# Last stage of a one-core decoder layer: a buffer for every tile, mixer tiles read during the stage before, one scaling on ScalarE

## The chip, the cores and the metric

The kernel runs on one NeuronCore of a Trainium2 chip. The metric is the device time of one execution in microseconds (us). The profile is one further execution with the hardware profiler on.

## The reference, cut to what matters

The program is one decoder layer over 2048 tokens of 1024 float32 numbers: a token mixer (pooling and dilated attention) and then a mixture of experts. Only the very end of it is touched:

```
# h: normalised rows after the mixer; x: the residual stream after the mixer
y = zeros(T, D).at[slot_tok].add(expert_out[slot] * slot_w[slot])   # two slots per token
x = x + gt_f * (y * rsqrt(mean(y * y, -1) + 1e-6) * g_post_ffn)
```

Each token has two experts, so two rows of the experts' output, each with its own share. The last stage fetches the two rows, adds them with their shares, normalises the sum, scales it by a row of 1024 numbers and adds the mixer's result.

## The kernel before

`build` calls the stages one after another; each stage is a scope that ends by clearing its semaphores and with a barrier of all engines. The last three are `route`, `experts` and `combine`. Intermediates lie in DRAM: `x1_dram` ("x_mixed", the residual stream after the mixer, 8.39 MB), `h_dram`, and `y_dram` ("y_slots", 64 blocks of 128 expert output rows, of which a run-time table says how many are used). `x1_dram` is written in the stage before `route`.

`experts` works block by block on 128 rows of one expert. Its weights come in 12 parts (`PARTS = 12`, of which `GU = 8` are gate/up parts) into `raw_gu` and `raw_d`, 12 times 128 x 1024 float32. ScalarE and VectorE cut each part into a high and a low half (L1479, L1485); when the low half of part g is done, `lo_ready[g]` goes up and SyncE may load the next expert's part over the raw one. When SyncE has issued the last expert's weights, it writes zeros to the unused blocks of `y_dram` (L1509) and waits until they have landed. ScalarE stores each block's output (L1639).

`combine` works on 16 tiles of 128 tokens with three buffers (`BUF = 3`) for each kind of tile:

- GpSimd gathers the two expert rows of each token into `yy[:, t % 3, 0]` and `yy[:, t % 3, 1]` by two indirect DMAs of 128 rows of 4 KB (L1730). From tile 3 on it first waits until VectorE has mixed tile t - 3.
- SyncE loads the row `mod` (broadcast to 128 partitions) and, two tiles ahead, the mixer's tile into `x1[:, t % 3]` (L1741). From tile 3 on this waits until the store out of that same buffer has landed. In its one queue the load of tile t + 2 stands ahead of the store of tile t (L1749).
- VectorE's `mix(t)` scales the first row by its share (L1769, tensor_scalar) and adds the second (L1771, scalar_tensor_tensor). Then for each tile: `mix(t + 1)`, the reciprocal of the root (L1780), the scaling by it and by `mod` (L1782), and the sum with the mixer's tile, written into `x1` (L1786).
- ScalarE squares the mixed tile with an accumulated sum (L1760) and takes the root (L1762).

The two lines that hold the waits in question:

```
if t >= BUF: pool.wait_ge(mixed, t - BUF + 1)                   # GpSimd, ahead of a tile's two gathers
if t >= BUF: sp.wait_ge(stored[t % BUF], 16 * (t // BUF))       # SyncE, ahead of a load of x1
```

Of the kernel before, what the change touches and what calls it, by code (L numbers as in the profile page):

```python
# [5 lines left out]
P = 128  # L6
D = 1024
SEQ = 2048
KD = D // P
TILES = SEQ // P  # L10
# [10 lines left out]
NE = EG * EPG  # L21
DE = 512
KE = DE // P
NB = 64
EPS = 1e-6

F32 = mybir.dt.float32
F32R = mybir.dt.float32r
I32 = mybir.dt.int32
ALU = mybir.AluOpType  # L30
ACT = mybir.ActivationFunctionType
AX = mybir.AxisListType
ds = bass.ds
# [913 lines left out]
NR = EG + NE  # L947
# [266 lines left out]
H2 = DE // 2  # L1214
GU, PARTS = 8, 12


def route(nc, logits, dest, share, table, slot_rows, raw_gu, raw_d, w_gate, w_up, w_down):


# [195 lines left out]
                dve.wait_ge(rows_ready, 1)  # L1416


def experts(nc, table, slot_rows, ident, h_dram, raw_gu, raw_d, w_gate, w_up, w_down, y_dram):

# [2 lines left out]
    with ExitStack() as ctx:  # L1425
# [22 lines left out]
        lo_taken = [s.sem(f"lo_taken{i}") for i in range(2)]  # L1448
        silu_ready = [s.sem(f"silu_ready{i}") for i in range(2)]
        hid_ready = [s.sem(f"hid_ready{i}") for i in range(2)]  # L1450
        row_ready, row_seen, all_stored, zeroed, rest_zeroed, y_ready = (s.sem(n) for n in (
            "row_ready", "row_seen", "all_stored", "zeroed", "rest_zeroed", "y_ready"))

        def entry(eng, r, b, top):
            return eng.value_load(table[0:1, r, ds(b, 1)], min_val=0, max_val=top)
# [31 lines left out]
        with nc.Block() as block:  # L1487
            @block.sync
            def _(sp):
                def load(e, before):  # L1490

                    for g in range(PARTS):
                        sp.wait_ge(lo_ready[g], before)
                        load_part(sp, g, e, raw_gu, raw_d, w_gate, w_up, w_down, part_loaded[g])

                for g in range(PARTS):
                    sp.sem_inc(part_loaded[g], 32 if g < GU else 16)  # L1497

                def reload(b):
                    with sp.If(entry(sp, 1, b, 1) > 0):  # L1500
                        load(entry(sp, 0, b, NE - 1), entry(sp, 2, b, NE))

                count = by_twos(sp, lambda i: [reload(2 * i), reload(2 * i + 1)])

                sp.wait_ge(zeroed, 1)
                with sp.Fori(0, NB // 2) as i:
                    with sp.If(2 * i >= count):
                        for u in range(2):
                            sp.dma_start(y_dram[ds((2 * i + u) * P, P), :], zero[:, :]).then_inc(rest_zeroed, 16)  # L1509
                    with sp.Else():  # L1510
                        sp.sem_inc(rest_zeroed, 32)
                sp.wait_ge(rest_zeroed, 16 * NB)

            @block.gpsimd
# [186 lines left out]
                by_twos(dve, lambda i: [block_of(2 * i, 0), block_of(2 * i + 1, 1)])  # L1701


def combine(nc, dest, share, y_dram, x1_dram, gate_dram, out):

    BUF = 3
    with ExitStack() as ctx:
        s = Scope(nc, ctx, "comb")
        yy = s.sb("yy", [P, BUF, 2, D])
        x1 = s.sb("x1", [P, BUF, D])  # L1710
        y = s.sb("y", [P, BUF, D])
        sq = s.sb("sq", [P, D])
        mod = s.sb("mod", [P, D])
        eps = s.sb("eps", [P, 1])
        ms, root, rstd = s.sb("ms", [P, 2]), s.sb("root", [P, 2]), s.sb("rstd", [P, 2])
        gathered = [s.sem(f"gathered{i}") for i in range(BUF)]
        x_loaded = [s.sem(f"x_loaded{i}") for i in range(BUF)]
        stored = [s.sem(f"stored{i}") for i in range(BUF)]
        mod_loaded, eps_ready, first, mixed, squared, rooted, recips, scaled, summed = (s.sem(n) for n in (
            "mod_loaded", "eps_ready", "first", "mixed", "squared", "rooted", "recips", "scaled", "summed"))  # L1720
        with nc.Block() as block:
            @block.gpsimd
            def _(pool):
                pool.memset(eps[:, :], EPS).then_inc(eps_ready, 1)  # L1724

                for t in range(TILES):
                    if t >= BUF:
                        pool.wait_ge(mixed, t - BUF + 1)
                    for c in range(2):
                        pool.indirect_dma_start(out=yy[:, t % BUF, c, :], out_offset=None, in_=y_dram,  # L1730
                                                in_offset=bass.IndirectOffsetOnAxis(ap=dest[:, c, t:t + 1], axis=0)
                                                ).then_inc(gathered[t % BUF], 16)

            @block.sync
            def _(sp):
                sp.dma_start(mod[:, :], gate_dram.partition_broadcast(P)).then_inc(mod_loaded, 16)

                def load(t):
                    if t >= BUF:
                        sp.wait_ge(stored[t % BUF], 16 * (t // BUF))  # L1740
                    sp.dma_start(x1[:, t % BUF, :], x1_dram[ds(t * P, P), :]).then_inc(x_loaded[t % BUF], 16)  # L1741

                load(0)
                load(1)
                for t in range(TILES):
                    if t + 2 < TILES:
                        load(t + 2)
                    sp.wait_ge(summed, t + 1)
                    sp.dma_start(out[0, ds(t * P, P), :], x1[:, t % BUF, :]).then_inc(stored[t % BUF], 16)  # L1749
                for i in range(BUF):  # L1750
                    sp.wait_ge(stored[i], 16 * len(range(i, TILES, BUF)))

            @block.scalar
            def _(act):
                act.wait_ge(eps_ready, 1)
                for t in range(TILES):
                    act.wait_ge(mixed, t + 1)
                    if t >= 2:
                        act.wait_ge(recips, t - 1)
                    nc.scalar.activation(sq[:, :], y[:, t % BUF, :], ACT.Square, accum_out=ms[:, t % 2:t % 2 + 1]).then_inc(squared, 1)  # L1760
                    act.wait_ge(squared, t + 1)
                    nc.scalar.activation(root[:, t % 2:t % 2 + 1], ms[:, t % 2:t % 2 + 1], ACT.Sqrt, scale=1.0 / D,  # L1762
                                         bias=eps[:, 0:1]).then_inc(rooted, 1)

            @block.vector
            def _(dve):
                def mix(t):
                    dve.wait_ge(gathered[t % BUF], 32 * (t // BUF + 1))
                    dve.tensor_scalar(y[:, t % BUF, :], yy[:, t % BUF, 0, :], share[:, 0, t:t + 1], None, ALU.mult).then_inc(first, 1)  # L1769
                    dve.wait_ge(first, t + 1)  # L1770
                    dve.scalar_tensor_tensor(out=y[:, t % BUF, :], in0=yy[:, t % BUF, 1, :], scalar=share[:, 1, t:t + 1],  # L1771
                                             in1=y[:, t % BUF, :], op0=ALU.mult, op1=ALU.add).then_inc(mixed, 1)

                dve.wait_ge(mod_loaded, 16)
                mix(0)
                for t in range(TILES):
                    if t + 1 < TILES:
                        mix(t + 1)
                    dve.wait_ge(rooted, t + 1)
                    dve.reciprocal(rstd[:, t % 2:t % 2 + 1], root[:, t % 2:t % 2 + 1]).then_inc(recips, 1)  # L1780
                    dve.wait_ge(recips, t + 1)
                    dve.scalar_tensor_tensor(out=y[:, t % BUF, :], in0=y[:, t % BUF, :], scalar=rstd[:, t % 2:t % 2 + 1],  # L1782
                                             in1=mod[:, :], op0=ALU.mult, op1=ALU.mult).then_inc(scaled, 1)
                    dve.wait_ge(scaled, t + 1)
                    dve.wait_ge(x_loaded[t % BUF], 16 * (t // BUF + 1))
                    dve.tensor_tensor(x1[:, t % BUF, :], y[:, t % BUF, :], x1[:, t % BUF, :], ALU.add).then_inc(summed, 1)  # L1786


def build(nc, x, c, w_ada, b_ada, g_pre_mix, g_post_mix, g_pre_ffn, g_post_ffn, w_in, w_pool_group, pool_scale,
# [13 lines left out]
    with ExitStack() as ctx:  # L1803
        def top(name, shape, dt=F32):
            return ctx.enter_context(nc.sbuf_tensor(name, shape, dt))
# [10 lines left out]
        merge(nc, proj, att, ident, w_pool_group, pool_scale, w_branch_pool, w_branch_att, merged)  # L1816
        dest, share = top("dest", [P, 2, TILES], I32), top("share", [P, 2, TILES])
        table, slot_rows = top("table", [1, 4, NB + 1], I32), top("slot_rows", [P, NB + 2], I32)
        with nc.sbuf_tensor("logits", [P, TILES, NR], F32) as logits:
            mix_out(nc, x, merged, w_out, ada_part, b_ada, (g_post_mix, g_pre_ffn, g_post_ffn), ident, w_group_router,  # L1820
                    w_expert_router, b_group_router, b_expert_router, gate_dram, x1_dram, h_dram, logits)
            with nc.sbuf_tensor("raw_gu", [P, GU, 2, 2, H2], F32) as raw_gu, nc.sbuf_tensor("raw_d", [P, KE, D], F32) as raw_d:
                route(nc, logits, dest, share, table, slot_rows, raw_gu, raw_d, w_exp_gate, w_exp_up, w_exp_down)
                experts(nc, table, slot_rows, ident, h_dram, raw_gu, raw_d, w_exp_gate, w_exp_up, w_exp_down, y_dram)
        combine(nc, dest, share, y_dram, x1_dram, gate_dram, out)


# [21 lines left out]
```

## Time and profile before

| | |
|---|---|
| time, median of 3 (lowest to highest) | 2801.63 us (2801.57 to 2801.66) |
| the profiled execution: its own time | 2803.04 us |
| its span, from first to last instruction | 2801.3 us |
| `combine` in it | from 2679 to 2801.3 us, 122 us |
| last expert output stored (issued) | 2672.6 us |

The span is the trace's time axis: 0 is the first instruction. The time of an execution is 1.7 us more than its span here. An engine's idle time is put down to whatever released it last; a load or a store "lands" when its last byte is there. DMA share is the mean busy share of the core's 16 DMA engines.

### The profile page before, as it was taken

To read this page: it belongs to the slowest core of one execution; us is meant where nothing else is said; L and a number is where in the kernel's file an instruction comes from. 1 tells how busy PE (TensorE), PEld (TensorE's weight loads), DVE (VectorE), ACT (ScalarE), POOL (GpSimd) and SP (SyncE) were. 2 spreads that over 40 slices of the span, in tenths; PEclk is the share of its full clock that TensorE was granted. 3 is DMA by queue.
4 is the path that set the end of the run, shared out by engine and by line. 5 is a ranking of instruction groups with operands and counts; after the bars stand their busy time and mean duration, and the time that the engine had idled before them with its cause. 6 is when DMAs were issued, how large, how long until landed. Compare 5 with 4: busy or idle time off the path is not lost. (4 is left out here: it accounts for less than half of the span.)

```text
span 2801.3 us, 39203 instructions
## 1 busy us (share of the span) xinstructions
PE 2397.4 (86%) x13485; PEld 2056.7 (73%) x13486; DVE 1365.5 (49%) x1700; ACT 917.5 (33%) x1509; POOL 474.8 (17%) x311
## 2 busy tenths in 40 slices
PE   3599999999999888868959983999999999999910
PEld 3488888888888677846848873888889889889910
DVE  6552111122323177646424447886664756466346
ACT  3200000000000055433322221886664755565321
POOL 2311111111111101022335541010010100010032
PEclk9799999999999999769979995999999999999955
DMA  6112212132332423255554433998975876678468
GB/s 224 46 60 90 75 60 75 60 111 102 132 124 101 162 99 109 81 166 200 200 197 158 151 135 127 368 375 300 323 258 207 289 272 231 240 254 296 184 224 270
DMA packets 293164, 499.73 MB, mean 178 GB/s; under 512 B 21337, under 2 KB 226673, under 8 KB 283506
## 3 DMA queue, kind: packets, MB, share of 16 engines
q1 hardware_dynamic: 269778, 414.05, 43.1%
q0 software_dynamic: 11808, 43.00, 4.6%
q10 hardware_dynamic: 11520, 41.95, 3.8%
q8 instruction: 32, 0.52, 0.1%
q14 instruction: 26, 0.21, 0.0%
HBM read 383.37 MB, written 115.54 MB: 178 GB/s over the span
## 5 line engine op out<-in xcount | busy, mean ns | idle before, releaser
L349 PE MATMUL proj_psum<-h_hi,proj_w_hi 128*128 128x512 f32 x1216 | 481.8, 396 | 19.1 <-POOL proj_w_lo L334 19.1
L350 PE MATMUL proj_psum<-h_lo,proj_w_hi 128*128 128x512 f32 x1216 | 481.6, 396 | 0.0
L351 PE MATMUL proj_psum<-h_hi,proj_w_lo 128*128 128x512 f32 x1216 | 481.4, 396 | 0.0
L1546 PE MATMUL moe_p_gu<-moe_hi_gu,moe_xT_hi 128*128 128x256 f32 x1536 | 440.5, 287 | 1.7 <-DVE moe_xT_lo L1660 1.7
L369 DVE COPY proj_out<-proj_psum 128x512 f32<-128x512 f32 x152 | 123.7, 815 | 635.3 <-PE proj_psum L351 634.1
L1547 PE MATMUL moe_p_gu<-moe_lo_gu,moe_xT_hi 128*128 128x256 f32 x1536 | 432.6, 282 | 0.0
L1548 PE MATMUL moe_p_gu<-moe_hi_gu,moe_xT_lo 128*128 128x256 f32 x1536 | 432.5, 282 | 0.0
L1485 DVE TENSOR_TENSOR moe_lo_gu<-raw_gu,moe_hi_gu 128x1024 fp32r<-128x1024 f32 x256 | 301.5, 1219 | 23.8 <-ACT moe_hi_gu L1479 17.4
L327 ACT ACTIVATE proj_w_hi<-proj_raw 128x1024 fp32r<-128x1024 f32 x38 | 40.3, 1061 | 781.9 <-PE proj_psum L351 772.2
L1546 PEld LDWEIGHTS moe_p_gu<-moe_hi_gu,moe_xT_hi 128*128 128x128 f32 x1536 | 290.5, 189 | 4.2 <-issue 2.1
L1547 PEld LDWEIGHTS moe_p_gu<-moe_lo_gu,moe_xT_hi 128*128 128x128 f32 x1536 | 290.7, 189 | 2.1
L1548 PEld LDWEIGHTS moe_p_gu<-moe_hi_gu,moe_xT_lo 128*128 128x128 f32 x1536 | 290.6, 189 | 0.0
L349 PEld LDWEIGHTS proj_psum<-h_hi,proj_w_hi 128*128 128x128 f32 x1216 | 228.9, 188 | 74.7 <-issue 19.5
L1479 ACT ACTIVATE moe_hi_gu<-raw_gu 128x1024 fp32r<-128x1024 f32 x256 | 256.5, 1057 | 41.1 <-SPq L1497 41.1
L350 PEld LDWEIGHTS proj_psum<-h_lo,proj_w_hi 128*128 128x128 f32 x1216 | 228.9, 188 | 55.4
L351 PEld LDWEIGHTS proj_psum<-h_hi,proj_w_lo 128*128 128x128 f32 x1216 | 228.9, 188 | 55.4
L334 POOL TENSOR_TENSOR proj_w_lo<-proj_raw,proj_w_hi 128x1024 fp32r<-128x1024 f32 x38 | 98.2, 2585 | 724.6 <-ACT proj_w_hi L327 724.6
L1546 PE MATMUL moe_p_y<-moe_hi_d,moe_hT_hi 128*128 128x512 f32 x384 | 159.4, 415 | 34.9 <-DVE moe_hT_lo L1660 34.9
L1681 DVE TENSOR_TENSOR moe_hid<-moe_p_gu,moe_act_g 128x256 f32<-128x256 f32 x96 | 40.6, 423 | 264.9 <-ACT moe_act_g L1621 264.2
L1518 POOL COPY moe_row<-slot_rows 128x1 int32 (+1 forms) x50 | 30.6, 612 | 801.2 <-PE moe_p_turn L1537 787.4
L1548 PE MATMUL moe_p_y<-moe_hi_d,moe_hT_lo 128*128 128x512 f32 x384 | 151.7, 395 | 0.0
L1547 PE MATMUL moe_p_y<-moe_lo_d,moe_hT_hi 128*128 128x512 f32 x384 | 151.5, 394 | 0.0
(261 smaller groups left out, 3791.9 us busy)
## 6 DMA issues: line engine op xcount, KB each, us to landing
raw_gu<-in_w_exp_gate SPq DMA_DIRECT2D x256, 256.0 KB, 6.3
raw_gu<-in_w_exp_up SPq DMA_DIRECT2D x256, 256.0 KB, 7.7
raw_d<-in_w_exp_down SPq DMA_DIRECT2D x128, 512.0 KB, 9.1
projected<-proj_out SPq DMA_DIRECT2D x38, 1024.0 KB, 4.3
y_slots<-moe_ys ACTq DMA_DIRECT2D x48, 512.0 KB, 6.4
proj_raw<-in_w_in SPq DMA_DIRECT2D x38, 512.0 KB, 6.2
att_qkv<-projected SPq DMA_DIRECT2D x18, 1024.0 KB, 8.4
proj_w_rest<-in_w_ada SPq DMA_DIRECT2D x8, 2048.0 KB
```

Of the source, the lines that this page charges most:

```text
L327: nc.scalar.activation(w_hi[:, u, :, :], raw[:, u, :, :], ACT.Copy).then_inc(hi_ready[u], 1)
L334: pool.tensor_tensor(w_lo[:, u, :, :], raw[:, u, :, :], w_hi[:, u, :, :], ALU.subtract).then_inc(lo_ready[u], 1)
L349: pe.matmul(bank, w_hi[:, u, k, :], h_hi[:, k, tok], start=(k == 0), stop=False)
L350: pe.matmul(bank, w_hi[:, u, k, :], h_lo[:, k, tok], start=False, stop=False)
L351: mm = pe.matmul(bank, w_lo[:, u, k, :], h_hi[:, k, tok], start=False, stop=(k == KD - 1))
L369: ins = dve.tensor_copy(view[:, ds(tg * per, per), :], psum[:, u, tg, :].rearrange("p (m r) -> p m r", r=dilation))
L1479: nc.scalar.activation(hi_part(g), raw_part(g), ACT.Copy).then_inc(hi_ready[g], 1)
L1485: dve.tensor_tensor(lo_part(g), raw_part(g), hi_part(g), ALU.subtract).then_inc(lo_ready[g], 1)
L1546: pe.matmul(bank, x_hi, w_hi, start=first, stop=False)
L1547: pe.matmul(bank, x_hi, w_lo, start=False, stop=False)
L1548: return pe.matmul(bank, x_lo, w_hi, start=False, stop=last)
L1681: dve.tensor_tensor(hid[:, half, :], p_gu[:, half, 1, 0:H2], act_g[:, half, :], ALU.mult).then_inc(hid_ready[half], 1)
```

## The change

1. `combine` holds all 16 tiles of gathered rows at once: `yy` is `[P, TILES, 2, D]`. GpSimd issues its 32 gathers without any wait. Each gather has a semaphore of its own. The buffers `y` are gone: everything is computed in place in `yy[:, t, 0]`, and the output is stored from there.
2. The mixer's tiles 0 to 11 are loaded in `experts`, by SyncE, after its zero blocks are issued, each into one of the 12 raw weight parts and each after the last expert's cut of that part (`lo_ready[g]`). SyncE leaves the stage when they have landed. `raw_gu`, `raw_d` (and `logits`) stay allocated to the end. Only tiles 12 to 15 (`LATE = 4`) are loaded in `combine`, at its start, into buffers of their own.
3. The first scaling (share 0) moves from VectorE to ScalarE as a Copy activation with a scale per partition, issued one tile ahead, ahead of the square of the tile before.
4. The constant `eps` is set by VectorE and not by GpSimd. `ms`, `root` and `rstd` have one column per tile. The one store semaphore is waited on once, at the end.

```
+def x1_part(t, raw_gu, raw_d):
+    return raw_gu[:, t, :, :, :].rearrange("p m k f -> p (m k f)") if t < GU else raw_d[:, t - GU, :]
...
 # experts, SyncE
+                cut = entry(sp, 2, NB, NE) + 1
+                for g in range(PARTS):
+                    sp.wait_ge(lo_ready[g], cut)
+                    sp.dma_start(x1_part(g, raw_gu, raw_d), x1_dram[ds(g * P, P), :]).then_inc(x1_loaded, 16)
+                sp.wait_ge(x1_loaded, 16 * PARTS)
                 sp.wait_ge(rest_zeroed, 16 * NB)
...
 # combine, GpSimd
-                pool.memset(eps[:, :], EPS).then_inc(eps_ready, 1)
                 for t in range(TILES):
-                    if t >= BUF:
-                        pool.wait_ge(mixed, t - BUF + 1)
                     for c in range(2):
-                        pool.indirect_dma_start(out=yy[:, t % BUF, c, :], out_offset=None, in_=y_dram,
+                        pool.indirect_dma_start(out=yy[:, t, c, :], out_offset=None, in_=y_dram,
                                                 in_offset=bass.IndirectOffsetOnAxis(ap=dest[:, c, t:t + 1], axis=0)
-                                                ).then_inc(gathered[t % BUF], 16)
+                                                ).then_inc(gathered[t][c], 16)
...
 # combine, SyncE
-                load(0)
-                load(1)
+                for t in range(LATE):
+                    sp.dma_start(x1[:, t, :], x1_dram[ds((PARTS + t) * P, P), :]).then_inc(x_loaded[t], 16)
                 for t in range(TILES):
-                    if t + 2 < TILES:
-                        load(t + 2)
                     sp.wait_ge(summed, t + 1)
-                    sp.dma_start(out[0, ds(t * P, P), :], x1[:, t % BUF, :]).then_inc(stored[t % BUF], 16)
+                    sp.dma_start(out[0, ds(t * P, P), :], yy[:, t, 0, :]).then_inc(stored, 16)
...
 # combine, ScalarE
+                def weight(t):
+                    act.wait_ge(gathered[t][0], 16)
+                    nc.scalar.activation(yy[:, t, 0, :], yy[:, t, 0, :], ACT.Copy, scale=share[:, 0, t:t + 1]).then_inc(first, 1)
+
                 act.wait_ge(eps_ready, 1)
+                weight(0)
                 for t in range(TILES):
+                    if t + 1 < TILES:
+                        weight(t + 1)
                     act.wait_ge(mixed, t + 1)
...
 # combine, VectorE
                 def mix(t):
-                    dve.wait_ge(gathered[t % BUF], 32 * (t // BUF + 1))
-                    dve.tensor_scalar(y[:, t % BUF, :], yy[:, t % BUF, 0, :], share[:, 0, t:t + 1], None, ALU.mult).then_inc(first, 1)
+                    dve.wait_ge(gathered[t][1], 16)
                     dve.wait_ge(first, t + 1)
-                    dve.scalar_tensor_tensor(out=y[:, t % BUF, :], in0=yy[:, t % BUF, 1, :], scalar=share[:, 1, t:t + 1],
-                                             in1=y[:, t % BUF, :], op0=ALU.mult, op1=ALU.add).then_inc(mixed, 1)
+                    dve.scalar_tensor_tensor(out=yy[:, t, 0, :], in0=yy[:, t, 1, :], scalar=share[:, 1, t:t + 1],
+                                             in1=yy[:, t, 0, :], op0=ALU.mult, op1=ALU.add).then_inc(mixed, 1)
```

## Rows read from the trace of the kernel before

**Rows 1.** The page's first line: the profiled execution.

```profile
span 2801.3 us, 39203 instructions
```

**Rows 2.** The chain that ended last, from 2690 us: start, length, what.

```profile
by line: DMA out<-comb_x 78.8%; DMA comb_yy<-y_slots,dest 8.1%; DMA comb_x<-x_mixed 3.8%; SPq L1741 3.4%; DVE comb_x L1786 2.2%; DVE comb_y L1782 1.2%; DVE comb_y L1771 1.2%; ACT L1760 1.1%; ACT L1762 1.1%; ACT comb_sq L1760 1.0%; issue 1.0
...
2681.09 9.07 DMA comb_yy<-y_slots,dest
...
2796.49 1.23 DVE comb_x L1786
```

**Rows 3.** Busy time by stretch: each engine, granted clock, DMA share, GB/s.

```profile
2679.00:2690.00 11.00, 0.00 (x0) 0.00 (x0) 0.00 (x0) 0.00 (x0) 5.72 (x7) 0.50 0.88 328
2685.00:2690.00 5.00, 0.00 (x0) 0.00 (x0) 0.00 (x0) 0.00 (x0) 1.70 (x2) 0.50 1.02 397
2690.00:2780.00 90.00, 0.00 (x0) 0.00 (x0) 59.90 (x66) 22.67 (x44) 37.92 (x26) 0.50 0.88 292
2710.00:2715.00 5.00, 0.00 (x0) 0.00 (x0) 3.88 (x6) 1.44 (x3) 3.90 (x2) 0.50 0.95 363
2730.00:2780.00 50.00, 0.00 (x0) 0.00 (x0) 31.72 (x35) 10.11 (x21) 18.16 (x13) 0.50 0.92 304
2780.00:2801.30 21.30, 0.00 (x0) 0.00 (x0) 12.87 (x14) 2.89 (x6) 0.00 (x0) 0.50 0.62 198
```

**Rows 4.** DMA from 2679 us on: packets; issues, KB each, median us to landing.

```profile
DMA packets 9362, 34.10 MB, mean 277 GB/s; under 512 B 1040, under 2 KB 1040, under 8 KB 9360
...
comb_x<-x_mixed SPq DMA_DIRECT2D x16, 512.0 KB, 5.6
```

**Rows 5.** Waits from 2679 us on: us in total, times, longest.

```profile
POOL comb_yy L1730 <- DVE comb_y L1771: 43.7, 12, 8.2
DVE comb_x L1786 <- DMA comb_x<-x_mixed: 31.3, 13, 6.7
```

**Rows 6.** Waits of SyncE's queue from 2560 us on.

```profile
SPq L1741 <- DMA out<-comb_x: 82.7, 13, 10.3
```

**Rows 7.** Groups of instructions from 2690 us on.

```profile
L1771 DVE SCALAR_TENSOR_TENSOR comb_y<-comb_yy,share,comb_y 128x1024 f32<-128x1024 f32 x16 | 20.5, 1284 | 0.6
...
L1760 ACT ACTIVATE comb_sq<-comb_y 128x1024 f32<-128x1024 f32 x16 | 16.9, 1056 | 71.7 <-DVE comb_y L1771 71.7
```

**Rows 8.** VectorE in order of time, one tile without a wait.

```profile
2701.17 0.15 DVE L1780 RECIPROCAL comb_rstd<-comb_root 128x1 f32<-128x1 f32 x1
...
2703.82 0.75 DVE L1769 TENSOR_SCALAR comb_y<-comb_yy,share 128x1024 f32<-128x1024 f32 x1
2704.60 1.28 DVE L1771 SCALAR_TENSOR_TENSOR comb_y<-comb_yy,share,comb_y 128x1024 f32<-128x1024 f32 x1
2705.80 0.15 DVE L1780 RECIPROCAL comb_rstd<-comb_root 128x1 f32<-128x1 f32 x1
```

**Rows 9.** GpSimd in order of time: a gather's issue alone, and beside VectorE.

```profile
2681.09 0.94 POOL L1730 DMA_INDIRECT comb_yy<-y_slots,dest  x1 [0.30 <-issue]
...
2701.52 1.93 POOL L1730 DMA_INDIRECT comb_yy<-y_slots,dest  x1 [2.70 <-DVE comb_y L1771]
```

**Rows 10.** SyncE's, VectorE's, GpSimd's and ScalarE's last work in `experts`.

```profile
2605.54 18.82 SPq L1509 DMA_DIRECT2D y_slots<-moe_zero  x16
...
2616.68 4.62 DVE L1485 TENSOR_TENSOR moe_lo_d<-raw_d,moe_hi_d 128x1024 fp32r<-128x1024 f32 x4
...
2631.69 0.97 POOL L1521 DMA_INDIRECT moe_xg<-h_moe,moe_row  x1 [0.79 <-POOL moe_row L1518]
...
2640.91 1.09 ACT L1600 ACTIVATE moe_xT_hi<-moe_p_turn 128x512 fp32r<-128x512 f32 x2
...
2672.61 0.34 ACTq L1639 DMA_DIRECT2D y_slots<-moe_ys  x1
```

**Rows 11.** Busy time by stretch at the end of `experts`.

```profile
2620.00:2630.00 10.00, 10.00 (x83) 9.78 (x82) 3.86 (x7) 2.13 (x5) 0.00 (x0) 1.00 1.02 417
...
2628.00:2645.00 17.00, 17.00 (x123) 15.88 (x123) 2.74 (x6) 4.94 (x8) 1.15 (x2) 1.00 0.29 114
2645.00:2672.00 27.00, 26.29 (x177) 23.68 (x175) 4.07 (x9) 5.01 (x10) 1.15 (x2) 1.00 0.10 39
```

More of the change, by code:

```diff
@@ L1416, in _, with experts @@
                 dve.wait_ge(rows_ready, 1)
-def experts(nc, table, slot_rows, ident, h_dram, raw_gu, raw_d, w_gate, w_up, w_down, y_dram):
+def experts(nc, table, slot_rows, ident, h_dram, raw_gu, raw_d, w_gate, w_up, w_down, y_dram, x1_dram):
     with ExitStack() as ctx:
@@ L1450, in experts @@
         hid_ready = [s.sem(f"hid_ready{i}") for i in range(2)]
-        row_ready, row_seen, all_stored, zeroed, rest_zeroed, y_ready = (s.sem(n) for n in (
-            "row_ready", "row_seen", "all_stored", "zeroed", "rest_zeroed", "y_ready"))
+        row_ready, row_seen, all_stored, zeroed, rest_zeroed, y_ready, x1_loaded = (s.sem(n) for n in (
+            "row_ready", "row_seen", "all_stored", "zeroed", "rest_zeroed", "y_ready", "x1_loaded"))
         def entry(eng, r, b, top):
@@ L1701, in _, with combine @@
                 by_twos(dve, lambda i: [block_of(2 * i, 0), block_of(2 * i + 1, 1)])
-def combine(nc, dest, share, y_dram, x1_dram, gate_dram, out):
-    BUF = 3
+def combine(nc, dest, share, y_dram, x1_dram, gate_dram, raw_gu, raw_d, out):
+    LATE = TILES - PARTS
     with ExitStack() as ctx:
         s = Scope(nc, ctx, "comb")
-        yy = s.sb("yy", [P, BUF, 2, D])
-        x1 = s.sb("x1", [P, BUF, D])
-        y = s.sb("y", [P, BUF, D])
+        yy = s.sb("yy", [P, TILES, 2, D])
+        x1 = s.sb("x1", [P, LATE, D])
         sq = s.sb("sq", [P, D])
@@ L1714, in combine @@
         eps = s.sb("eps", [P, 1])
[L1715 to L1720, printed above, removed]
+        ms, root, rstd = s.sb("ms", [P, TILES]), s.sb("root", [P, TILES]), s.sb("rstd", [P, TILES])
+        gathered = [[s.sem(f"gathered{t}_{c}") for c in range(2)] for t in range(TILES)]
+        x_loaded = [s.sem(f"x_loaded{t}") for t in range(LATE)]
+        mod_loaded, eps_ready, first, mixed, squared, rooted, recips, scaled, summed, stored = (s.sem(n) for n in (
+            "mod_loaded", "eps_ready", "first", "mixed", "squared", "rooted", "recips", "scaled", "summed", "stored"))
         with nc.Block() as block:
@@ L1736, in _ @@
                 sp.dma_start(mod[:, :], gate_dram.partition_broadcast(P)).then_inc(mod_loaded, 16)
[L1738 to L1741, printed above, removed]
-                load(0)
-                load(1)
+                for t in range(LATE):
+                    sp.dma_start(x1[:, t, :], x1_dram[ds((PARTS + t) * P, P), :]).then_inc(x_loaded[t], 16)
                 for t in range(TILES):
-                    if t + 2 < TILES:
-                        load(t + 2)
                     sp.wait_ge(summed, t + 1)
-                    sp.dma_start(out[0, ds(t * P, P), :], x1[:, t % BUF, :]).then_inc(stored[t % BUF], 16)
-                for i in range(BUF):
-                    sp.wait_ge(stored[i], 16 * len(range(i, TILES, BUF)))
+                    sp.dma_start(out[0, ds(t * P, P), :], yy[:, t, 0, :]).then_inc(stored, 16)
+                sp.wait_ge(stored, 16 * TILES)
             @block.scalar
             def _(act):
+                def weight(t):
+                    act.wait_ge(gathered[t][0], 16)
+                    nc.scalar.activation(yy[:, t, 0, :], yy[:, t, 0, :], ACT.Copy, scale=share[:, 0, t:t + 1]).then_inc(first, 1)
                 act.wait_ge(eps_ready, 1)
+                weight(0)
                 for t in range(TILES):
+                    if t + 1 < TILES:
+                        weight(t + 1)
                     act.wait_ge(mixed, t + 1)
-                    if t >= 2:
-                        act.wait_ge(recips, t - 1)
-                    nc.scalar.activation(sq[:, :], y[:, t % BUF, :], ACT.Square, accum_out=ms[:, t % 2:t % 2 + 1]).then_inc(squared, 1)
+                    if t:
+                        act.wait_ge(squared, t)
+                    nc.scalar.activation(sq[:, :], yy[:, t, 0, :], ACT.Square, accum_out=ms[:, t:t + 1]).then_inc(squared, 1)
                     act.wait_ge(squared, t + 1)
-                    nc.scalar.activation(root[:, t % 2:t % 2 + 1], ms[:, t % 2:t % 2 + 1], ACT.Sqrt, scale=1.0 / D,
+                    nc.scalar.activation(root[:, t:t + 1], ms[:, t:t + 1], ACT.Sqrt, scale=1.0 / D,
                                          bias=eps[:, 0:1]).then_inc(rooted, 1)
@@ L1767, in mix @@
                 def mix(t):
-                    dve.wait_ge(gathered[t % BUF], 32 * (t // BUF + 1))
-                    dve.tensor_scalar(y[:, t % BUF, :], yy[:, t % BUF, 0, :], share[:, 0, t:t + 1], None, ALU.mult).then_inc(first, 1)
+                    dve.wait_ge(gathered[t][1], 16)
                     dve.wait_ge(first, t + 1)
-                    dve.scalar_tensor_tensor(out=y[:, t % BUF, :], in0=yy[:, t % BUF, 1, :], scalar=share[:, 1, t:t + 1],
-                                             in1=y[:, t % BUF, :], op0=ALU.mult, op1=ALU.add).then_inc(mixed, 1)
+                    dve.scalar_tensor_tensor(out=yy[:, t, 0, :], in0=yy[:, t, 1, :], scalar=share[:, 1, t:t + 1],
+                                             in1=yy[:, t, 0, :], op0=ALU.mult, op1=ALU.add).then_inc(mixed, 1)
+                dve.memset(eps[:, :], EPS).then_inc(eps_ready, 1)
                 dve.wait_ge(mod_loaded, 16)
@@ L1779, in _ @@
                     dve.wait_ge(rooted, t + 1)
-                    dve.reciprocal(rstd[:, t % 2:t % 2 + 1], root[:, t % 2:t % 2 + 1]).then_inc(recips, 1)
+                    dve.reciprocal(rstd[:, t:t + 1], root[:, t:t + 1]).then_inc(recips, 1)
                     dve.wait_ge(recips, t + 1)
-                    dve.scalar_tensor_tensor(out=y[:, t % BUF, :], in0=y[:, t % BUF, :], scalar=rstd[:, t % 2:t % 2 + 1],
+                    dve.scalar_tensor_tensor(out=yy[:, t, 0, :], in0=yy[:, t, 0, :], scalar=rstd[:, t:t + 1],
                                              in1=mod[:, :], op0=ALU.mult, op1=ALU.mult).then_inc(scaled, 1)
                     dve.wait_ge(scaled, t + 1)
-                    dve.wait_ge(x_loaded[t % BUF], 16 * (t // BUF + 1))
-                    dve.tensor_tensor(x1[:, t % BUF, :], y[:, t % BUF, :], x1[:, t % BUF, :], ALU.add).then_inc(summed, 1)
+                    if t >= PARTS:
+                        dve.wait_ge(x_loaded[t - PARTS], 16)
+                        mixer_out = x1[:, t - PARTS, :]
+                    else:
+                        mixer_out = x1_part(t, raw_gu, raw_d)
+                    dve.tensor_tensor(yy[:, t, 0, :], yy[:, t, 0, :], mixer_out, ALU.add).then_inc(summed, 1)
 def build(nc, x, c, w_ada, b_ada, g_pre_mix, g_post_mix, g_pre_ffn, g_post_ffn, w_in, w_pool_group, pool_scale,
@@ L1818, in build @@
         table, slot_rows = top("table", [1, 4, NB + 1], I32), top("slot_rows", [P, NB + 2], I32)
[L1819 to L1825, printed above, removed]
+        logits = top("logits", [P, TILES, NR])
+        mix_out(nc, x, merged, w_out, ada_part, b_ada, (g_post_mix, g_pre_ffn, g_post_ffn), ident, w_group_router,
+                w_expert_router, b_group_router, b_expert_router, gate_dram, x1_dram, h_dram, logits)
+        raw_gu, raw_d = top("raw_gu", [P, GU, 2, 2, H2]), top("raw_d", [P, KE, D])
+        route(nc, logits, dest, share, table, slot_rows, raw_gu, raw_d, w_exp_gate, w_exp_up, w_exp_down)
+        experts(nc, table, slot_rows, ident, h_dram, raw_gu, raw_d, w_exp_gate, w_exp_up, w_exp_down, y_dram, x1_dram)
+        combine(nc, dest, share, y_dram, x1_dram, gate_dram, raw_gu, raw_d, out)
 _INS = ["x", "c", "w_ada", "b_ada", "g_pre_mix", "g_post_mix", "g_pre_ffn", "g_post_ffn", "w_in", "w_pool_group",
```

## The prediction, as put on record before the change was run

> **What bounds the kernel now.** Only the last stage and the end of the one before it are touched, so I read the views for those alone. First the chain that ended last [rows 2]. From 2690 us on it is almost nothing but transfers: 78.8% of it is "the store of an output tile must land", then the next load of a mixer tile is issued, then the next store. The reader is to see that no engine stands in it but for 1 to 2% each. Second, the waits [rows 5, 6]: SyncE stood 82.7 us for stores before it could reload their buffer, VectorE 31.3 us for mixer tiles, GpSimd 43.7 us for buffers. It looks like a chain of too few buffers. Third, the busy time by stretch [rows 3], which says something else: from 2690 to 2780 us the 16 DMA engines were busy 88% of the time, and 92% from 2730 to 2780, at 304 GB/s. The waits are long because each transfer shares the DMA engines with the others. Idle engines are left mainly at the end, 62% from 2780 on. So the stage is bound first by the bytes it moves and only then by its waits. The DMA view counts the bytes [rows 4]: 34.10 MB. A tile of 128 x 1024 float32 is 0.524 MB, and 32 gathers, 16 mixer tiles, 16 stores and the broadcast row are 65 of them, 34.1 MB, which agrees.
>
> **The change part by part.**
>
> *Twelve mixer tiles leave the stage.* 12 x 0.524 = 6.29 MB. What is left in it is 34.10 - 6.29 = 27.81 MB. At the 304 GB/s of [rows 3] the removed bytes alone are 20.7 us.
>
> *They are loaded in the experts stage instead.* SyncE's queue: 16 zero blocks are issued from 2605.5 to 2624.4 us, and only then the 12 loads. Their wait is for the cuts of the last expert's weights; the last of these ends at 2616.7 + 4.6 = 2621.3 us [rows 10], so all 12 waits are already met. Nothing is queued behind these waits on SyncE but the end of the stage. At the 417 GB/s of the zero stores [rows 11] the loads take 15.1 us; behind what is left of the zeros they have landed by 2645 us, or by 2650 if the rate is the 304 of the last stage. The stage cannot end before its last output block, issued at 2672.6 us [rows 10]: at least 22 us of cover. The DMA engines have room, 0.29 from 2628 to 2645 and 0.10 from there to 2672 [rows 11]. What could be late is the gather of an expert block's rows, issued at 2632.7 and read by the transposes ahead of the copy at 2640.9 [rows 10]: some 8 us. With half of 304 GB/s its 0.524 MB take 3.4 us. I cost it at nothing. Bounds: no gain, since TensorE fills this stretch; a loss of at most 5 us, if a backlog of about 4 MB stood before that gather (13 us at 304).
>
> *Gathers without waits.* An issue takes 0.94 + 0.30 = 1.24 us alone and 1.93 us beside VectorE [rows 9]. In the worst case 8 at 1.24 and 24 at 2.23 us, 64 us, ending near 2744; in the best near 2720. Either is ahead of the transfers, as the next paragraph has the last gather landing at 2764. So the 43.7 us of waiting go, and what they give is that the DMA engines always have gathers queued. The late tiles 12 to 15 and the row are 2.62 MB at the start against 2.10 before; their queue only takes its share beside the gathers, so I leave the first pair's landing at 2690.2 us [rows 2]. Moving the memset off GpSimd gives at most 0.7 us, which I leave out.
>
> *Stores no longer bar loads.* The chain of stores and loads is gone. A store is late for nobody, except the last.
>
> *The first scaling on ScalarE.* I take the square's 1.06 us for the 128x1024 Copy [rows 7]; bounds 0.75 us (what VectorE needs, [rows 8]) and 1.3 us. ScalarE then has 1.06 + 1.06 + about 0.5 us a tile, 2.6. VectorE's tile took 2705.80 - 2701.17 = 4.63 us without waits, of which 2704.60 - 2703.82 = 0.78 go [rows 8]: 3.85 us. 16 tiles are 62 us. Both are below what the transfers need, so this is worth nothing now; it decides what limits the stage if the transfers become fast.
>
> *The sum.* From 2679 to 2690.3 us as before: 328 GB/s x 11 us = 3.61 MB [rows 3]. Stores that come after the last gather has landed: two tiles, 1.05 MB. Between lie 27.81 - 3.61 - 1.05 = 23.15 MB. The rate is the disputed number. Bounds from the rows: 292 GB/s, the mean with the stalls in it, gives 79.3 us; 363, the best mixed stretch of 5 us, gives 63.8 us [rows 3]. If the 8% of idle DMA time between 2730 and 2780 us went wholly, the rate would be 304 / 0.92 = 330. I can't see whether these 8% are waits or the slower ones of the 16 engines, so I take 312, a third of the way: 74.2 us. The last gather lands at 2764.5. Then VectorE mixes tile 15 (1.3 us), finishes tile 14 and tile 15 (2.65 us each: 3.85 less the start-to-start 1.20 of the mix, [rows 8]), and the last store lands as it did, 2801.3 - 2797.7 = 3.6 us after the sum [rows 1, 2]: 10.2 us. The span ends at 2774.7, 26.6 us earlier. The profiled execution took 2803.04 us, the median of the runs shown is 1.41 less; 2801.63 - 26.6 = 2775.0 us.
>
> The HBM Reference of the Trainium skill (section Specifications) says that a core streaming alone gets about 425 GB/s, bounded by its 16 DMA engines, and about 358 only when its neighbour streams too. No mixed stretch of this stage shows that; the nearest are 397 and 417 GB/s for loads alone or stores alone [rows 3, 11]. At 425 the middle term would be 54.5 us, less than VectorE's work.
>
> **The rivals.**
>
> *A: bytes bound the stage, the DMA engines are kept fed (forecast).* 2766 to 2779 us, chance 0.60.
>
> *B: deep queues bring the rate up and VectorE becomes the bound.* For it: 397 GB/s at share 1.02 from 2685 to 2690 us, with loads and gathers only [rows 3]; 23.15 MB at 397 are 58.3 us, under VectorE's 61.6. Against it: with stores mixed in, no 5 us passed 363. Then the end is 2690.3 + 61.6 + about 2.5 (first tile's chain) + 3.6 = 2758; the time about 2758. A mix of both cases, at 363, ends at 2764.3. The skill's 425 GB/s would end the same way. Chance 0.15 for 2757 to 2766.
>
> *C: the buffers bring nothing, only the bytes count.* The share stays where it was because transfers wait for one another and not for buffers; then the gain is the 20.7 us of the removed bytes, 2781 us; at 280 GB/s for the middle term, 2783. For it: 0.92 already with the waits in place. Against it: the thin ends. Chance 0.19 for 2779 to 2790.
>
> *D: slower.* The preload holds up the end of the experts stage. SyncE leaves only when all 12 tiles have landed. Each us beyond some 2676 us is added to the time, and it outweighs the 26.6 us if they land after about 2703. They would have to be issued 50 us later than the queue view says. The order in the queue (zeros, then loads) and the cuts done at 2621.3 speak against it. At 60 us late the time would be about 2810. Chance 0.02.
>
> *E: the change doesn't do what it says,* since the queue that the gathers use takes only a few at a time, so GpSimd is held inside its instructions. Six were issued before the first had been used, at 1.24 us each, so it takes six at least; the DMA engines would stay fed and the time would be that of C. It has the remaining 0.04, spread over both signs of no change (2795 to 2807) as well.
>
> **How the numbers follow.** 2775.0 us is that of A. The range leaves out the fast half of B and the slow end of C, D and E: 2761 to 2786 us. What can be told from no change here is about 0.2%, 5.6 us. Faster than that: A, B, C and most of E, 0.95; within it 0.03; slower 0.02.
>
> **What would show it right or wrong.** In the profile after: some 27.8 MB from the start of the last stage on, and a DMA share of 0.9 to 1.0 until the last gather; the first mix at 2690 us after a stage start at 2679; gathers issued by 2720 to 2744; 12 loads of mixer tiles issued at about 2625 us and TensorE without a new wait up to 2672; VectorE idle about 0.8 us a tile for gathers, and none of the chain's links a load. B would show VectorE without idle time and its operations in the chain; C a share at 0.9 or below with the gathers all queued; D the last stage beginning later than 2679. The forecast is wrong if the rate with both queues full is not 290 to 345 GB/s.

## The result, and the profile after

The changed kernel takes 2760.01 us (median of 4, 2753.18 to 2761.03) beside 2801.64 us before: ratio 0.9844, 95% interval 0.9826 to 0.9861, 41.6 us less. The prediction was 2775 us, range 2761 to 2786; the sign is right, the gain was put at two thirds of what it is (26.6 us), and the measured time lies 1 us outside the range. The number is that of rival B, "about 2758".

The first line of the changed kernel's page, and its chain by line from 2650 us on (the shares are of 150 us):

```profile
span 2759.2 us, 39211 instructions
...
by line: DVE comb_yy L1771 11.1%; ACT comb_yy L1751 8.3%; ACT comb_sq L1761 7.6%; issue 7.2%; DMA comb_yy<-y_slots,dest 6.9%; DVE comb_yy L1783 6.0%; DVE comb_yy L1791 1.7%; POOL comb_yy L1733 1.2%; DVE comb_rstd L1781 0.4%; ACT comb_root L
```

The chain that was nearly all stores [rows 2] is now VectorE and ScalarE, with no store in it. Of the two, VectorE is the one without slack: from 2696.2 us on it has no gap, while the fourth mix, at 2702.7 us, uses a Copy of ScalarE that had ended at 2699.6. Busy time by stretch, once from 2690 to 2740 us and then where the transfers run out; the columns are those of [rows 3]:

```profile
2690.00:2740.00 50.00, 0.00 (x0) 0.00 (x0) 45.57 (x48) 33.73 (x55) 24.53 (x24) 0.50 1.03 417
...
2740.00:2750.00 10.00, 0.00 (x0) 0.00 (x0) 9.85 (x10) 5.06 (x9) 0.00 (x0) 0.50 0.43 172
```

The DMA engines moved 417 GB/s with gathers, loads and stores mixed, where the kernel before had 304 [rows 3]. Then they run out of work while VectorE is still busy without a gap. DMA from 2679 us on, and VectorE's and SyncE's waits (three views; the last two list who waited for whom, us in total, times, longest). The mean of 226 GB/s in the first is over a window of 123 us that runs past the end of the span; only its bytes are used here:

```profile
DMA packets 7634, 27.81 MB, mean 226 GB/s; under 512 B 848, under 2 KB 848, under 8 KB 7632
```

```profile
DVE comb_yy L1771 <- DMA comb_yy<-y_slots,dest: 13.4, 2, 11.6
```

```profile
SPq L1744 <- DVE comb_yy L1791: 51.5, 11, 17.7
...
SPq L1491 <- DMA raw_d<-x_mixed: 15.8, 1, 15.8
```

VectorE waits for gathers twice, for the first tile and for the second. SyncE's 82.7 us of waiting for stores [rows 6] are gone; it waits for VectorE. Its 15.8 us for the preloaded tiles lie in the stage before, under TensorE's work.

The order of time in the changed kernel, SyncE, then the first two mixes and the last tile on VectorE:

```profile
2605.31 19.03 SPq L1513 DMA_DIRECT2D y_slots<-moe_zero  x16
2626.05 5.57 SPq L1519 DMA_DIRECT2D raw_gu<-x_mixed  x8
2631.66 1.88 SPq L1519 DMA_DIRECT2D raw_d<-x_mixed  x4
2678.78 0.33 SPq L1739 DMA_DIRECT2D comb_mod<-gate_ffn  x1
```

```profile
2690.51 1.28 DVE L1771 SCALAR_TENSOR_TENSOR comb_yy<-comb_yy,share 128x1024 f32<-128x1024 f32 x1 [11.59 <-DMA comb_yy<-y_slots,dest]
2693.60 1.28 DVE L1771 SCALAR_TENSOR_TENSOR comb_yy<-comb_yy,share 128x1024 f32<-128x1024 f32 x1 [1.81 <-DMA comb_yy<-y_slots,dest]
...
2752.89 1.28 DVE L1783 SCALAR_TENSOR_TENSOR comb_yy<-comb_yy,comb_rstd,comb_mod 128x1024 f32<-128x1024 f32 x1
2754.21 1.23 DVE L1791 TENSOR_TENSOR comb_yy<-comb_yy,comb_x 128x1024 f32<-128x1024 f32 x1
```

I call the stretch from the issue of the broadcast row to the span's end "the stage". (Where the row is loaded earlier, in e8 and e9, I count from 0.1 us before VectorE's first memset, since in the changed kernel the row is issued that much ahead of it.) It was 2801.3 - 2679.1 = 122.2 us and is 2759.2 - 2678.8 = 80.4 us. The difference, 41.8 us, is the whole gain between these two profiles; nothing moved ahead of the stage (the last output block is issued at 2672.2 us, 2672.6 before).

### The profile page after: what moved, and what is told of

Same layout as the page of the kernel before. It is cut to its first block and busy times, and to the rows that moved or that the text cites. A ratio compares the mean times of both kernels' runs of the same rounds, so it can differ in the third digit from the quotient of the medians.

```text
span 2759.2 us, 39211 instructions
## 1 busy us (share of the span) xinstructions
PE 2398.3 (87%) x13485; PEld 2056.1 (75%) x13486; DVE 1353.4 (49%) x1685; ACT 934.2 (34%) x1525; POOL 463.0 (17%) x310
## 5 line engine op out<-in xcount | busy, mean ns | idle before, releaser
L350 PEld LDWEIGHTS proj_psum<-h_lo,proj_w_hi 128*128 128x128 f32 x1216 | 228.9, 188 | 55.5
L351 PEld LDWEIGHTS proj_psum<-h_hi,proj_w_lo 128*128 128x128 f32 x1216 | 228.8, 188 | 55.5
```

The source lines that it names most:

```text
L350: pe.matmul(bank, w_hi[:, u, k, :], h_lo[:, k, tok], start=False, stop=False)
L351: mm = pe.matmul(bank, w_lo[:, u, k, :], h_hi[:, k, tok], start=False, stop=(k == KD - 1))
```

## The experiments

The stage starts anywhere from 2671 to 2682 us in the profiles below (a spread of 10 us, not the 13 that one expectation names), also where the edit touches nothing ahead of it, and the times scatter with it. So each experiment has the stage's length, from one profile, beside its time. Every ratio is against the kernel before, run beside it. In the three sets of runs for the experiments (11, 19 and 7 runs) that kernel had medians of 2795.7, 2795.6 and 2795.3 us, and not the 2801.6 of the four runs beside the changed kernel. Against these the changed kernel's 2760.0 us are some 36 us less, not 41.6, a ratio of about 0.987; rows of different sets are compared by the stage.

| kernel | stage, us | time, us | ratio, 95% interval |
|---|---|---|---|
| before | 122.2, again 119.6 | 2801.6; again, one run, 2801.5 | |
| changed | 80.4, again 80.4 | 2760.0; again, one run, 2758.0 | 0.9844, 0.9826 to 0.9861 |
| e1 gathers at most 3 tiles ahead | 80.6 | 2759.8 | 0.9870, 0.9834 to 0.9907 |
| e2 no preload | 92.3 | 2770.5 | 0.9911, 0.9886 to 0.9937 |
| e3 preload only | 92.0 | 2767.1 | 0.9906, 0.9874 to 0.9939 |
| e4 first scaling on VectorE | 92.3 | 2770.4 | 0.9905, 0.9874 to 0.9936 |
| e5 before, 16 mixer buffers | 95.8 | 2775.2 | 0.9919, 0.9887 to 0.9950 |
| e6 before, store ahead of load | 95.7 | 2774.5 | 0.9925, 0.9903 to 0.9947 |
| e7 before, scaling on ScalarE | 113.9 | 2796.2 | 1.0008, 0.9986 to 1.0029 |
| e10 = e6 and e7 | 96.4 | 2774.1 | 0.9913, 0.9884 to 0.9943 |
| e8 changed, shorter head | 78.6 | 2759.3 | 0.9863, 0.9833 to 0.9894 |
| e9 = e8, two tiles more preloaded, shorter tail | 75.1 | 2757.7 | 0.9859, 0.9829 to 0.9889 |

**e1: is it the depth of the gather queue?** In the changed kernel GpSimd waits again:

```
 for t in range(TILES):
+    if t >= 3: pool.wait_ge(mixed, t - 2)
```

> The changed kernel, but GpSimd waits ahead of a tile's gathers until tile t - 3 is mixed, so at most three tiles are queued, as before the change. Theory 'depth' (the DMA engines reach 415 GB/s instead of 304 only because many gathers stand in their queue): the rate falls back towards 304 to 330 GB/s and the time rises to 2770 to 2777 us. Theory 'loads' (what slowed the transfers before was the chain in which each mixer load waits for a store, and the mixer loads beside the gathers; three tiles of gathers are deep enough): the rate stays above 380 GB/s while VectorE needs data, and the time stays within 3 us of the changed kernel's 2760.

Neither stage (80.6 us beside 80.4) nor time changes, though GpSimd waits 16.1 us and the rate is lower:

```profile
POOL comb_yy L1735 <- DVE comb_yy L1773: 16.1, 13, 5.7
```

```profile
2690.00:2740.00 50.00, 0.00 (x0) 0.00 (x0) 46.28 (x50) 33.44 (x53) 35.16 (x26) 0.50 0.99 381
```

"Depth" falls. Freeing the 32 gathers from their waits is worth nothing here; three tiles ahead are enough for VectorE.

**e2: the preload, with all buffers kept.** All 16 mixer tiles are loaded at the start of the last stage into `x1 = s.sb("x1", [P, TILES, D])`; nothing is loaded in `experts`.

> The changed kernel without the preload: all 16 mixer tiles are loaded at the start of the last stage, without waits, into buffers of their own; the stage moves 34.1 MB again. Theory 'depth': 415 GB/s holds with mixer loads in the mix as well, 34.1 MB take 82 us from 2679.5 us on, end 2764 to 2769 us, time about 2767. Theory 'loads': mixer loads beside gathers bring the rate back to about 310 GB/s, 110 us, time 2790 to 2795.

The 34.1 MB run at 415 GB/s for 70 us; now VectorE waits for gathers, 25.7 us in 11 waits against 13.4 in 2:

```profile
2680.00:2750.00 70.00, 0.00 (x0) 0.00 (x0) 51.97 (x54) 39.41 (x60) 24.50 (x26) 0.50 1.03 415
```

```profile
DVE comb_yy L1766 <- DMA comb_yy<-y_slots,dest: 25.7, 11, 11.7
```

The stage is 92.3 us. Mixer loads beside gathers don't slow the transfers. Both theories as first put ("depth", "loads beside gathers") are wrong in one half: what is left is the chain of waits.

**e3: the preload alone.** `combine` of the kernel before, tiles 0 to 11 read from the raw parts and stored from there; three gather buffers and the scaling on VectorE kept.

```
-load(0); load(1); ... load(t + 2) behind a wait for a store
+for t in range(PARTS, TILES): sp.dma_start(mixer(t), x1_dram[ds(t * P, P), :]).then_inc(x_loaded[t - PARTS], 16)
```

> The kernel before with the preload alone: mixer tiles 0 to 11 read from the raw weight parts, 12 to 15 loaded at the stage's start; three gather buffers with their waits, the first scaling on VectorE, y buffers as before. No store has anything to wait behind it. Theory 'depth': rate about 304 to 330, the middle 23.15 MB take 70 to 76 us, time 2772 to 2778. Theory 'loads': the rate rises to 380 or more and VectorE with 4.63 us a tile is the bound, 16 x 4.63 = 74 us, time 2770 to 2772; the two are told apart by VectorE's idle time between tiles: 5 to 15 us in all under 'depth', under 3 us under 'loads'.

The time, 2767.1, is a little under both expectations, but VectorE's idle time decides: it waits for transfers for the first tile and the second and never after (24.2 us in 2 waits; 23.0 are the first, counted from its last work in the stage before). Its busy time by stretch is the most useful row of this study:

```profile
2700.00:2750.00 50.00, 0.00 (x0) 0.00 (x0) 48.87 (x55) 15.88 (x33) 28.87 (x20) 0.50 0.96 337
```

VectorE is the bound, 4.63 us a tile, and asks for 1.57 MB / 4.63 us = 340 GB/s. It gets them (my 380 for "loads" overlooked that VectorE wouldn't ask for more), and the DMA share still reads 0.96. The same engines move 417 GB/s at 1.03. So a share of 0.92 at 304 GB/s was no sign that the engines were at their limit.

**e4: the first scaling back on VectorE**, in the changed kernel.

> The changed kernel with the first scaling back on VectorE (tensor_scalar, 0.75 us, 0.78 start to start). If VectorE bounds the changed kernel: 16 x 0.78 = 12.5 us more, time 2772 to 2773. If the transfers bound it (my prediction before the run): no change beyond 2 us. If the tensor_scalar holds GpSimd's descriptor writing up, gathers beside it take over 1.5 us each and their issue ends after 2730 us.

11.9 us more of stage, 16 x 0.78 = 12.5 expected: VectorE bounds the changed kernel. The third branch did not come: the last gather is issued at 2720.3 us, not after 2730, and the two issues that begin under a tensor_scalar take 0.93 and 0.94 us, as alone. (One issue in three does take 1.6 to 1.7 us, under another operation; see the last section.) VectorE is as busy while the transfers run at 418 GB/s as when they are down to 105:

```profile
2720.00:2730.00 10.00, 0.00 (x0) 0.00 (x0) 9.79 (x11) 2.89 (x6) 1.71 (x2) 0.50 1.03 418
```

```profile
2740.00:2750.00 10.00, 0.00 (x0) 0.00 (x0) 9.79 (x11) 3.61 (x7) 0.00 (x0) 0.50 0.26 105
```

**e5 and e6: the chain in SyncE's queue**, in the kernel before. e5 gives the loads 16 buffers, so that none waits for a store. e6 adds nothing and exchanges two steps:

```
 for t in range(TILES):
-    if t + 2 < TILES: load(t + 2)      # waits for the store of tile t - 1
     sp.wait_ge(summed, t + 1)
     sp.dma_start(out[...], x1[:, t % BUF, :]).then_inc(stored[t % BUF], 16)
+    if t + 2 < TILES: load(t + 2)
```

> The kernel before with 16 mixer buffers in place of three: a load is still issued two tiles ahead but waits for no store. Three gather buffers, the scaling on VectorE and all 34.1 MB stay. The stage took 122 us before. Theory 'chain' (the stage before was set by SyncE's queue: each store stood behind a load that waited for the store before it to land, 6.5 us a tile; the DMA engines were not saturated at 304 GB/s although their share read 0.92): the stage falls to 90 to 98 us, bound by the 34.1 MB at up to 415 GB/s (82 us) and VectorE's 74 us. Theory 'shallow mix' (loads, stores and few gathers side by side give only 300 to 330 GB/s): 34.1 MB take 105 us and more, the stage 110 to 118 us.

> The kernel before with one pair of lines exchanged in SyncE's queue: the store of tile t is issued ahead of the load of tile t + 2. Nothing else changes. Theory 'chain': the store no longer stands behind a load's wait. What is left is the loop of one mixer buffer, load 5.6 us, sum 1.2 us, store 6.2 us and 0.5 us of issuing over three tiles, 4.5 us a tile, so the stage falls from 122 us to 92 to 104 us. Theory 'shallow mix': the bytes and the queues' contents are as before, the stage stays within 4 us of 122.

Both as "chain" has it: 95.8 and 95.7 us, from some 120 to 122. The ten runs of e6 reach from 2769.3 to 2791.0 us, so here above all it is the stage that decides. In e6 SyncE's wait for stores (82.7 us before, [rows 6]) is 12.5 us, VectorE's for mixer tiles (31.3 us, [rows 5]) is 5.8, and the same 34.1 MB through the same three buffers run at 416 GB/s once the first tiles are through:

```profile
SPq L1741 <- DMA out<-comb_x: 12.5, 11, 1.6
```

```profile
DVE comb_x L1786 <- DMA comb_x<-x_mixed: 5.8, 9, 1.8
```

```profile
2710.00:2760.00 50.00, 0.00 (x0) 0.00 (x0) 44.12 (x50) 13.16 (x28) 27.59 (x18) 0.50 1.03 416
```

**e7: the scaling on ScalarE alone**, in the kernel before; **e10** with e6's exchange as well; and the two kernels profiled again.

> The kernel before with the first scaling on ScalarE alone. VectorE's tile falls from 4.63 to 3.85 us, but VectorE does not bound the stage before, under either theory: the stage stays at 122 us within 2 us. If it falls by 10 us or more, VectorE was in the chain.

> The kernel before, unchanged, for a second profile of its last stage (122.2 us in the first). The stage's start differed by up to 13 us between the profiles so far, so lengths of the stage are compared beside times. If the stage again takes 120 to 124 us, then the 113.9 us of the kernel with the scaling on ScalarE alone were a gain of that edit; if it takes some 114 to 118, its length differs from execution to execution and that edit was worth little.

> The changed kernel, unchanged, for a second profile: if VectorE sets its stage, the length is 80.4 us again within 0.5 us, since VectorE's durations hardly differ; if transfers set it, it may differ by several us as the kernel before may.

> The kernel before with the store ahead of the load in SyncE's queue and the first scaling on ScalarE: no buffer added, 34.1 MB in the stage. With the store first alone the stage took 95.7 us, VectorE having 4.63 us a tile, 74 us. With 3.85 us a tile VectorE needs 62 us, but 34.1 MB at 415 GB/s need 82 us: the transfers bound it, 91 to 95 us. If it falls to 86 or less, the transfers are faster than any stretch so far shows.

e7's stage is 113.9 us, shorter than I expected, but its time shows no gain (ratio 1.0008), and the kernel before's own stage came out 2.6 us shorter the second time. A chain of landing transfers differs from execution to execution; the changed kernel's stage is 80.4 us both times, as a chain of VectorE's work should be. I can't say whether part of the 6 us to e7 is real; landing stores are still 71% of its chain from 2690 us on. e10 is no better than e6: with VectorE's tile 0.78 us shorter nothing is gained, so VectorE doesn't bound these two. Its 96.4 us lie 1.4 us above the range I gave. Its transfers run at 406 GB/s from 2710 to 2760 us, near the 415 to 420, so that the 34.1 MB are the likely bound; but it still has three mixer buffers, and a load (7.1 us), the sum and a store (6.5 us) through each of them give about 5 us a tile as well. No run separates these two.

**e8 and e9: shorter than the changed kernel.** e8 loads the broadcast row in `experts`, issues the four late mixer tiles behind the first four stores, and loads ScalarE's table (1.28 us) early by a root of a constant. e9 preloads two of those four as well and puts the product with the row ahead of the root:

```
 # mix(t), VectorE
+    dve.wait_ge(mixed, t + 1)
+    dve.tensor_tensor(yy[:, t, 1, :], yy[:, t, 0, :], mod[:, :], ALU.mult).then_inc(scaled, 1)
...
 # last operation of a tile
-    scalar_tensor_tensor(yy0 * rstd * mod); tensor_tensor(+ mixer tile)
+    scalar_tensor_tensor(out=yy[:, t, 0, :], in0=yy[:, t, 1, :], scalar=rstd, in1=mixer_out, op0=mult, op1=add)
```

> The changed kernel with a shorter head: the broadcast row is loaded in the experts stage, the late mixer tiles are issued behind the first four stores, and ScalarE computes one root of a constant before the first gather has landed, so that its table is loaded by then. From the stage's start to the first tile's mix the changed kernel took 11.7 us. If the other loads share the DMA engines with the first gathers, 3 to 5 us of it go, and the table load takes 1.3 to 2.6 us off the first tile; the rest is bound by VectorE, 61.6 us, and the bytes, 27.3 MB at 415 GB/s, 66 us. Stage 80.4 us before, 73 to 76 after. If the head is the latency of a gather and not its bandwidth, only the table load shows, 78 to 79 us.

> The kernel with the shorter head (stage 78.6 us), and two changes more: two of the four late mixer tiles are loaded in the experts stage as well, into a buffer of their own, and VectorE multiplies by the row right after the mix, into the second gathered buffer, so that the last operation of a tile is one scalar_tensor_tensor with the root's reciprocal and the mixer's tile. VectorE's time a tile stays 3.85 us. In the kernel with the shorter head VectorE stood about 5 us for gathers in the middle of the stage, with the DMA engines at 418 to 420 GB/s: it moves 27.3 MB, now 26.2 MB (63 us at 415). If transfers and VectorE bound it together, the stage falls to 74 to 76 us. If it stays at 78 or more, the bytes taken out were not what VectorE waited for.

In e8 the first mix comes 7.2 us after the stage's start and not 11.7; yet the stage is only 1.8 us shorter: 78.6, not the 73 to 76 that I expected from a shorter head. In the middle VectorE waits for gathers again (12.5 us in all, 7.2 of them the first):

```profile
2710.00:2720.00 10.00, 0.00 (x0) 0.00 (x0) 7.77 (x9) 4.91 (x9) 7.56 (x9) 0.50 1.03 420
```

So with the shorter head the bytes bind for a time, at 420 GB/s. e9 takes 1.05 MB out and wins 3.5 us more, inside what was expected. It changes the order on VectorE too, and the two weren't tried apart; VectorE's waits for gathers fall from 12.5 to 9.3 us, which is most of the 3.5 and speaks for the bytes. Its stage is 5.3 us shorter than the changed kernel's; its time, 2757.7 us beside the 2760.0 of other runs, doesn't separate the two, whose intervals overlap.

## Why the prediction was wrong

*What bounds the kernel: read wrongly.* I took the views in the right order, met the right chain first, and then let the DMA share overrule it. "The waits are long because each transfer shares the DMA engines with the others" is the sentence that fails. e6 exchanges two steps and some 25 us go, with not a byte less. In SyncE's queue the store of tile t stood behind the load of tile t + 2, which waited for the store of t - 1 to land: one store's landing (median 6.2 us) and some 0.4 us of issuing for each tile. In e6 a store takes no less to land (6.5 us) while the engines move 416 GB/s; it only has no other store waiting behind it.

*The rate: the step that failed.* "The rate is the disputed number ... I take 312." It was 417. The upper bound, 363, was the best 5 us of a stretch that was starved itself, so no bound. My 304 / 0.92 = 330 took the share for a measure of the capacity left; e3 has 337 GB/s at 0.96 with the transfers waiting for VectorE. At 417 GB/s the middle term of 23.15 MB is 55.5 us and not 74.2, less than VectorE's 61.6, and the sum goes over to B: 2758, measured 2760.0. Two numbers had spoken for B and I gave them too little: 397 GB/s for loads and gathers, 417 for stores. B's own reason, deep queues, fell too: e1 and e6 reach 410 to 416 GB/s with gathers at most three tiles ahead. What had held it at 304 was the chain of stores. The HBM Reference of the Trainium skill (section Specifications) has about 425 GB/s for a core streaming alone. The traces come within 3% of it: 417 GB/s over 50 us in the changed kernel, 415 over 70 us in e2, 416 over 50 us in e6.

*The bytes removed: right as bytes, wrong as a price.* 27.81 MB were moved, to the digit. But no edit alone was worth the 20.7 us that I gave them at 304 GB/s. From the full change, undoing the preload costs 11.9 us (e2), undoing the ScalarE scaling 11.9 us (e4), undoing the gathers' freedom 0.2 us (e1). From the kernel before, the exchange of two steps gives about 24 to 26.5 us (e6), the preload 28 to 30 (e3), the scaling nothing measurable in the time (e7). The parts don't add up, since each wins only until the next bound: the store chain at 120, then bytes (92 to 96, 34.1 MB) or VectorE at 4.63 us a tile (92), then VectorE at 3.85 us (80).

*"The first scaling on ScalarE ... worth nothing now": wrong with the rate.* It is worth 11.9 us in place. The Copy takes 1.14 us (1.06 taken).

*Preload under the experts: right.* Issued at 2626.1 to 2633.5 us (2625 forecast), landed by about 2649 (2645 to 2650 forecast), no new wait of TensorE, stage start where it was. Rival D had no part in it.

*Gathers: right on the first pair (2690.5 us, 2690.2 forecast) and on the last issue being no bound.* It came at 2720.5, the best case: beside VectorE most issues took 0.93 to 1.04 us, three were longer, up to 1.95, where the forecast had 1.93 for its worst case. *The tail:* 2759.2 - 2755.4 = 3.8 us from the last sum to the end, 3.6 forecast.

## What to carry to other kernels

When a chain of waits and a high DMA share compete as the explanation, compare the GB/s with the highest rate that any stretch reached, and not the share with 1: shares of 0.92 to 0.96 stood beside 304 and 337 GB/s where 417 were possible. Look in each queue for an instruction without a dependence behind one that waits; exchanging the two cost no memory and gave over half of the gain here. And price an edit under each bound that may come next, since an edit "worth nothing now" is worth its full length when another edit lifts the bound above it.

## What the runs showed of the hardware

- The 16 DMA engines move 415 to 420 GB/s with 4 KB gathers from DRAM, loads and stores mixed, as fast as stores alone (417, [rows 11]).
- Their busy share reads 0.92 at 304 GB/s, 0.96 at 337 and 1.03 at 417: it tells little of what is left.
- A gather's issue takes 0.94 us alone; beside VectorE it depends on the moment (0.94 to 1.04 us mostly in the changed kernel, 1.67 in e4 for every third). The row there, issued 0.42 us into an operation with two SBUF inputs that ends at 2702.65, is done 0.81 us after that end, as is the one of [rows 9], done at 2703.45 beside an operation that ended at 2702.64 in that trace. The same holds of all 36 issues of over 1 us in the traces before, after and of e4: each began under a VectorE operation with two SBUF inputs and is done 0.80 to 0.82 us after that operation's end.

```profile
2701.79 1.67 POOL L1733 DMA_INDIRECT comb_yy<-y_slots,dest  x1 [0.31 <-issue]
```

```profile
2701.37 1.28 DVE L1766 SCALAR_TENSOR_TENSOR comb_yy<-comb_yy,share 128x1024 f32<-128x1024 f32 x1
```

  That the issue waits for the operation was read from these rows and not tried by itself; the SBUF page of the Trainium skill ("SBUF — State Buffer", section Who interferes with whom) says that such operations contend with a GpSimd instruction that reads SBUF. The 36 issues agree with it.
